# Matmuls without a reader on TensorE in the norms and at the layer edges of a two-block transformer kernel

## The chip, the cores and the metric

The kernel is one program on one core of a Trainium2 chip. Its metric is the device time of one launch in microseconds (us), of which the median over several executions counts. TensorE (PE in the profile) does the matmuls, VectorE (DVE), ScalarE (ACT) and GpSimd (POOL) the elementwise work, and SyncE (SP) starts the DMAs.

## The reference

Two blocks of two layers each work on 512 tokens of 1024 features, in float32. Each layer begins with an RMS norm, and each MLP, and the gate at the end of a layer of the first block, has a norm of its own:

```python
def _rms_norm(x, g):
    xf = x.astype(jnp.float32)
    y = xf * lax.rsqrt(jnp.mean(xf * xf, axis=-1, keepdims=True) + EPS) * g.astype(jnp.float32)

for l in range(DEPTH):                       # first block, DEPTH = 2
    h = _rms_norm(x, in_norm_g[l]); y = h @ w_in[l] + b_in[l]
    ...                                      # mLSTM, HGRN2 and sliding-window attention
    x = x + jnp.concatenate([m_out, h_out, s_out], axis=-1) @ w_out[l]
    u = _rms_norm(x, mlp_norm_g[l]) @ w_up[l]
    x = x + jnp.square(jax.nn.relu(u)) @ w_down[l]
    gate = jax.nn.sigmoid(_rms_norm(x, ple_norm_g[l]) @ w_ple_gate[l])
    x = x + gate * _rms_norm(p[l] @ w_ple_proj[l], ple_post_norm_g[l])
for layer in range(DEPTH):                   # second block
    h = rmsnorm(x, g_attn[layer]) * (1.0 + scale1) + shift1
    x = x + gate1 * mixer_layer(h, w_in[layer], ...)
    h = rmsnorm(x, g_mlp[layer]) * (1.0 + scale2) + shift2
    x = x + gate2 * (gated convolved MLP of h)
return rmsnorm(x, g_final)
```

That makes eleven norms over the whole of x: three per layer of the first block, two per layer of the second, and the last one.

## The kernel before

The activations x stay in SBUF as 8 chunks of 128 features by 512 tokens. Every dense product is made of three matmuls in place of one: weights and activations are split into a high and a low part (fp32r), and high times high, high times low and low times high are summed in PSUM. Weights come in panels of 1 MB; ScalarE writes a panel's high part (L291) and VectorE its low part (L303).

A layer of the first block is four blocks of code (`nc.Block`): the mixer (in `layer_one`), `mlp_one`, `embedding_gate` and `clear_semaphores`. A layer of the second is `layer_two`, `mlp_two` and `clear_semaphores`. Each kind of layer is the body of a hardware loop of two turns (L510 and L1641). At the end of each block of code each engine drains (a DRAIN in its queue) and then all wait for one another; in the profile these instructions bear the line of the `with nc.Block()` (L631, L1394, L1523 for the end of `embedding_gate`, L2163 for that of `mlp_two`, L209 for that of `clear_semaphores`). `clear_semaphores` sets some 60 to 130 semaphores to zero, a fifth of them on each engine; TensorE's are line 233.

A norm crosses such an end. While the last products of a block are added to x, ScalarE squares each chunk (L337) and GpSimd sums the squares (L349). TensorE sums over the partitions with 8 short matmuls (`sum_partitions`, L355 and L358), and its block ends there. In the next block ScalarE takes the root (`root_of_mean`, L362), VectorE the reciprocal (L367), and TensorE, which waits for that, spreads the result over all partitions (`spread_rstd`, L375). Then VectorE scales chunk after chunk (L401), ScalarE makes the high part (L388), VectorE the low part (L408 or L410), and TensorE's first two dense groups (`project_as_ready`, L434) take each chunk when it is ready: 48 matmuls. After that TensorE goes on with L420, L445 and the others.

For the first norm of a layer, `clear_semaphores` and the jump of the loop lie between the sum and the root, and VectorE splits a weight panel between the chunks (L303, before chunks 1 and 4 of the scaling). In `embedding_gate` TensorE's first products after the spread are those of the embedding (L420 on `ple_p_high`), which wait for a DMA, a copy and a subtraction (L1564, L1599).

Of the kernel before, what the change touches and what calls it, by code (L numbers as in the profile page):

```python
# [21 lines left out]
P = 128  # L22
# [180 lines left out]
        return self.made[name]  # L203

def clear_semaphores(nc, s):

    sems = list(s.made.values())
    with nc.Block() as block:  # L209
        @block.gpsimd  # L210
        def _(pool):
            for sem in sems[0::5]:
                pool.sem_clear(sem)

        @block.sync
        def _(sp):
            for sem in sems[1::5]:
                sp.sem_clear(sem)

        @block.vector  # L220
        def _(dve):
            for sem in sems[2::5]:
                dve.sem_clear(sem)

        @block.scalar
        def _(act):
            for sem in sems[3::5]:
                act.sem_clear(sem)

        @block.tensor  # L230
        def _(pe):
            for sem in sems[4::5]:
                pe.sem_clear(sem)

class Panels:
# [115 lines left out]
def sum_partitions(nc, pe, g, e):  # L352
    pe.wait_ge(e.sum_used, DC - 1)
    for t in range(NT):
        nc.tensor.matmul(g.bank[0][:, t:t + 1], g.rstd[:, 1, t * P:(t + 1) * P], g.ones[:, 0:1], start=t == 0, stop=False)  # L355
    pe.wait_ge(e.sq_ready, DC)
    for t in range(NT):
        nc.tensor.matmul(g.bank[0][:, t:t + 1], g.sq[:, (DC - 1) % 2, t * P:(t + 1) * P], g.ones[:, 0:1], start=False, stop=t == NT - 1)  # L358
# [9 lines left out]
    dve.wait_ge(e.rstd_spread, 1)  # L368

def spread_rstd(nc, pe, g, e):

    pe.wait_ge(e.rstd_ready, 1)
    for t in range(NT):
        ins = nc.tensor.matmul(g.bank[0][:, t * P:(t + 1) * P], g.by_token[:, NT + t:NT + t + 1].broadcast_to([P, P]), g.ident, start=True, stop=True)  # L375
    ins.then_inc(e.rstd_spread, 1)

def norm_scalar(nc, act, g, e, high, shift=None, before=None, shifts_ready=None):
# [134 lines left out]
def layer_one(nc, g, a, s, pan, l, k1, vec, row, gb, cs, lb, lsel, small):  # L514
    bank, x, nb = g.bank, g.x, g.nb
    with ExitStack() as ctx:
# [81 lines left out]
        e, nx = NormSignals(s, "in"), NormSignals(s, "mlp")  # L598
# [32 lines left out]
        with nc.Block() as block:  # L631
# [16 lines left out]
            def _(pe):  # L648
# [175 lines left out]
                        ins = nc.tensor.transpose(bank[7][:, t * P:(t + 1) * P], mix_chunk(c, t), g.ident)  # L824
                    ins.then_inc(chunk_turned, 1)

                spread_rstd(nc, pe, g, e)
                for i in range(n_before):
                    dense(i)
                for k in range(n_levels):  # L830
# [534 lines left out]

    mlp_one(nc, g, s, pan, l, vec)
    embedding_gate(nc, g, a, s, pan, l, vec)
    clear_semaphores(nc, s)

def mlp_one(nc, g, s, pan, l, vec):
# [134 lines left out]
def embedding_gate(nc, g, a, s, pan, l, vec):  # L1506
# [5 lines left out]
    e, ee, nx = NormSignals(s, "ple"), NormSignals(s, "emb"), NormSignals(s, "in")  # L1512
    with ExitStack() as ctx:
# [9 lines left out]
        with nc.Block() as block:  # L1523
            @block.sync
            def _(sp):
                sp.dma_start(pT[:, :, :], a["p1"][l, :, :, :]).then_inc(s("ple_in"), 16)
                pan.loads(sp, l, first + AHEAD, first + 5 + AHEAD)
                pan.load_next_layers(sp, l)

            @block.tensor  # L1530
            def _(pe):
                spread_rstd(nc, pe, g, e)
                w = pan.parts(pe, first)
                pe.wait_ge(s("p_low"), 1)
                for c in range(DC):
                    grp.free(pe, c)
                    project_feature(nc, pe, w, c * P, (ph, pl), grp.bank(g, c), kts=2).then_inc(full, 1)
                for c in range(DC):
                    w = pan.parts(pe, first + 1 + c // 2)
                    grp.free(pe, DC + c)  # L1540
                    if c == 0:
                        grp.free(pe, DC + 1)
                        project_as_ready(nc, pe, w, (hh, hl), [grp.bank(g, DC), grp.bank(g, DC + 1)], full, e.h_ready)
                    if c >= 2:
                        project_feature(nc, pe, w, (c % 2) * P, (hh, hl), grp.bank(g, DC + c)).then_inc(full, 1)
                    if c == 0:
                        pe.wait_ge(ee.sum_used, DC)
                        nc.tensor.matmul(g.bank[7][:, :], g.ones, erstd[:, 1, :], start=True, stop=True).then_inc(s("emb_total"), 1)
                sum_partitions(nc, pe, g, nx)

            @block.gpsimd
            def _(pool):
                for c in range(1, DC):
                    pool.wait_ge(ee.sq_ready, c + 1)
                    if c > 1:
                        pool.wait_ge(ee.sum_used, c)
                    nc.gpsimd.tensor_tensor(erstd[:, 1, :], esq[:, 0, :] if c == 1 else erstd[:, 1, :], esq[:, c, :], ALU.add).then_inc(ee.sum_used, 2 if c == 1 else 1)
                add_squares(nc, pool, g, nx)

            @block.scalar  # L1560
            def _(act):
                def p_high():
                    act.wait_ge(s("ple_in"), 16)
                    nc.scalar.activation(ph[:, :, :], pT[:, :, :], ACT.Copy).then_inc(s("p_high"), 1)  # L1564

                def embedding(c):
                    act.wait_ge(full, c + 1)
                    nc.scalar.activation(emb[:, c, :], grp.bank(g, c)[:, :], ACT.Copy).then_inc(s("emb_kept"), 1)
                    act.wait_ge(s("emb_kept"), c + 1)
                    nc.scalar.activation(esq[:, c, :], emb[:, c, :], ACT.Square).then_inc(ee.sq_ready, 1)  # L1570

                norm_scalar(nc, act, g, e, hh, before={0: p_high, 2: lambda: embedding(0), 3: lambda: embedding(1), 4: lambda: embedding(2),
                                                       5: lambda: embedding(3), 6: lambda: embedding(4), 7: lambda: embedding(5)})
                embedding(6)
                embedding(7)
                pan.high(act, first + 2)
                pan.high(act, first + 3, full, DC)
                for c in range(DC):
                    if c == 2:
                        pan.high(act, first + 4, full, DC + 2)  # L1580
                    act.wait_ge(full, DC + c + 1)
                    if c >= 2:
                        act.wait_ge(s("x_gated"), c - 1)
                    nc.scalar.activation(gate[:, c % 2, :], grp.bank(g, DC + c)[:, :], ACT.Sigmoid).then_inc(s("gate_kept"), 1)
                    if c == 0:
                        act.wait_ge(s("emb_total"), 1)
                        nc.scalar.activation(erstd[:, 0, :], g.bank[7][:, :], ACT.Sqrt, bias=g.eps, scale=1.0 / D).then_inc(ee.root_ready, 1)
                    if c >= 1:
                        act.wait_ge(s("x_gated"), c)
                        square_chunk(nc, act, g, nx, c - 1, x[:, c - 1, :])  # L1590
                act.wait_ge(s("x_gated"), DC)
                square_chunk(nc, act, g, nx, DC - 1, x[:, DC - 1, :])

            @block.vector
            def _(dve):
                st = Steps(s("ple_steps")).on(dve)
                def p_low():
                    dve.wait_ge(s("p_high"), 1)
                    nc.vector.tensor_tensor(pl[:, :, :], pT[:, :, :], ph[:, :, :].bitcast(F32), ALU.subtract).then_inc(s("p_low"), 1)  # L1599

                norm_vector(nc, dve, g, e, x, vec[:, V_GPLE:V_GPLE + DC], hh, hl, before={0: p_low})
                pan.low(dve, first + 2)
                dve.wait_ge(ee.root_ready, 1)
                st.link(nc.vector.reciprocal(erstd[:, 1, :], erstd[:, 0, :]))
                pan.low(dve, first + 3)
                for c in range(DC):
                    if c == 2:
                        pan.low(dve, first + 4)
                    st(nc.vector.scalar_tensor_tensor(emb[:, c, :], emb[:, c, :], vec[:, V_GPOST + c:V_GPOST + c + 1], erstd[:, 1, :], ALU.mult, ALU.mult))
                    dve.wait_ge(s("gate_kept"), c + 1)  # L1610
                    st.settle()
                    st.link(nc.vector.tensor_tensor(gate[:, c % 2, :], gate[:, c % 2, :], emb[:, c, :], ALU.mult))
                    nc.vector.tensor_tensor(x[:, c, :], x[:, c, :], gate[:, c % 2, :], ALU.add).then_inc(s("x_gated"), 1)
# [57 lines left out]
def layer_two(nc, g, a, s, pan, l, k2, vec, row, fb, mod, small):  # L1671
    bank, x, nb = g.bank, g.x, g.nb
    with ExitStack() as ctx:
# [90 lines left out]
        e = NormSignals(s, "in")  # L1764
# [18 lines left out]
        with nc.Block() as block:  # L1783
# [16 lines left out]
            def _(pe):  # L1800
# [90 lines left out]
                        ins = nc.tensor.transpose(bank[7][:, t * P:(t + 1) * P], mix_chunk(c, t), g.ident)  # L1891
                    ins.then_inc(chunk_turned, 1)

                spread_rstd(nc, pe, g, e)
                for i in range(n_before):
                    dense(i)
                for i in range(n_steps):
# [234 lines left out]
                    dense(i)  # L2132

    mlp_two(nc, g, s, pan, l, vec, mod)
    clear_semaphores(nc, s)

def mlp_two(nc, g, s, pan, l, vec, mod):
# [15 lines left out]
    e, nx = NormSignals(s, "mlp"), NormSignals(s, "in")  # L2154
    with ExitStack() as ctx:
# [7 lines left out]
        with nc.Block() as block:  # L2163
# [6 lines left out]
            def _(pe):  # L2170
                spread_rstd(nc, pe, g, e)
                for i, (half, kind, c, part) in enumerate(calls):
# [18 lines left out]
                                                   start=part == 0 and k == 0 and q == 0, stop=part == 1 and k == rows[1] - 1 and q == 2)  # L2191
                    ins.then_inc(full, 1)
                sum_partitions(nc, pe, g, nx)

            @block.gpsimd
            def _(pool):
# [226 lines left out]
```

## Time and profile before

| | |
|---|---|
| runs | 3159.9, 3160.41, 3169.08 us; median 3160.41 |
| profiled execution | 3157.43 us, span 3155.6 us |
| mean granted TensorE clock | 0.951 of full |
| PE busy | 2879.8 us (91%), 14756 matmuls |
| DVE busy | 1667.7 us (53%) |
| ACT busy | 1106.7 us (35%) |
| POOL busy | 108.0 us (3%) |
| DMA | 89 GB/s on average |

The granted clock is a share of full speed: 1.00 is 2.4 GHz and 0.50 is 1.2 GHz, and the chip grants TensorE no other level in this trace. A row of the timeline gives the start, the time from the start of the first to the end of the last of a merged group, the engine, the line, the operation, and in brackets how long the engine was idle before it and what ended that. The end of a matmul's record is modelled: two matmuls that follow one another overlap in the records, and the distance of their starts is what each costs.

### The profile page before, as it was taken

The numbers are of one execution on the slowest core, as the hardware profiler recorded it, in microseconds if no ns is written. First come the engines' busy times: TensorE is split into PE (matmuls) and PEld (weight loads), VectorE is DVE, ScalarE is ACT, GpSimd is POOL, SyncE is SP. The second block draws the span as 40 slices with busy tenths as digits, with TensorE's granted clock in tenths as the row PEclk, the third lists the DMA queues.
The fourth block names the chain that finished last, engine by engine and source line by source line (L and its number), as shares of the span: only waits on it lengthen the run. The fifth ranks groups of instructions, "written<-read, shape, count | busy, mean of one in ns | idle before, by whom it ended". The sixth has DMA issues, their size and how long they took to land. (4 is left out here: it accounts for less than half of the span.)

```text
span 3155.6 us, 37966 instructions
## 1 busy us (share of the span) xinstructions
PE 2879.8 (91%) x14756; PEld 2346.2 (74%) x14756; DVE 1667.7 (53%) x3011; ACT 1106.7 (35%) x1691; POOL 108.0 (3%) x88
## 2 busy tenths in 40 slices
PE   4798999999787989999996998899998998999998
PEld 3676778887666867888875887788886786778886
DVE  3656575555657555656655544553444544454442
ACT  4334332223453343222243444332332344332231
POOL 1000000000200000000020000000000000000000
PEclk9988899999888978999998999999998999999999
DMA  3110144443121102444422210132322210122322
GB/s 133 64 44 27 47 143 158 160 160 140 60 81 45 54 27 75 166 160 173 153 80 95 81 40 28 54 107 75 110 77 94 81 53 19 64 81 82 112 77 77
DMA packets 42993, 280.86 MB, mean 89 GB/s; under 512 B 5944, under 2 KB 6200, under 8 KB 11704
## 3 DMA queue, kind: packets, MB, share of 16 engines
q1 hardware_dynamic: 42808, 278.34, 25.4%
q8 instruction: 122, 2.00, 0.2%
q14 instruction: 63, 0.52, 0.1%
HBM read 276.23 MB, written 2.10 MB: 88 GB/s over the span
## 5 line engine op out<-in xcount | busy, mean ns | idle before, releaser
L303 DVE TENSOR_TENSOR low_panels<-raw_panels,high_panels 128x2048 fp32r<-128x2048 f32 (+3 forms) x218 | 469.2, 2153 | 345.1 <-ACT high_panels L291 345.0
L291 ACT ACTIVATE high_panels<-raw_panels 128x2048 fp32r<-128x2048 f32 (+3 forms) x218 | 392.5, 1801 | 494.9 <-PE bank L1419 150.6
L420 PE MATMUL bank<-mlp_h_high,high_panels 128*128 128x512 f32 x1152 | 457.3, 397 | 0.0
L420 PE MATMUL bank<-mlp_h_low,high_panels 128*128 128x512 f32 x1152 | 455.2, 395 | 0.0
L420 PE MATMUL bank<-mlp_h_high,low_panels 128*128 128x512 f32 x1152 | 455.1, 395 | 0.0
L420 PEld LDWEIGHTS bank<-mlp_h_high,low_panels 128*128 128x128 f32 x1152 | 216.1, 188 | 52.6
L420 PEld LDWEIGHTS bank<-mlp_h_low,high_panels 128*128 128x128 f32 x1152 | 216.2, 188 | 51.5
L420 PEld LDWEIGHTS bank<-mlp_h_high,high_panels 128*128 128x128 f32 x1152 | 216.2, 188 | 51.5
L445 PE MATMUL bank<-high_panels,h_high 128*128 128x256 f32 x704 | 211.6, 301 | 13.3 <-DVE arena L1100 12.7
L420 PE MATMUL bank<-h_high,high_panels 128*128 128x512 f32 x496 | 207.7, 419 | 12.9 <-DVE arena L1080 12.8
L1419 PE MATMUL bank<-mlp_hid_high,high_panels 128*128 128x512 f32 x512 | 204.5, 399 | 0.0
L445 PE MATMUL bank<-low_panels,h_high 128*128 128x256 f32 x704 | 202.4, 287 | 0.0
L1419 PE MATMUL bank<-mlp_hid_low,high_panels 128*128 128x512 f32 x512 | 202.4, 395 | 0.0
L1419 PE MATMUL bank<-mlp_hid_high,low_panels 128*128 128x512 f32 x512 | 202.3, 395 | 0.0
L445 PE MATMUL bank<-high_panels,h_low 128*128 128x256 f32 x704 | 201.6, 286 | 0.0
L420 PE MATMUL bank<-h_low,high_panels 128*128 128x512 f32 x496 | 199.1, 401 | 0.0
L420 PE MATMUL bank<-h_high,low_panels 128*128 128x512 f32 x496 | 198.4, 400 | 0.0
L1480 DVE SCALAR_TENSOR_TENSOR mlp_mod_acc<-raw_panels,conditioning,mlp_mod_acc 128x256 f32<-128x256 f32 x336 | 165.1, 491 | 12.0
L445 PEld LDWEIGHTS bank<-high_panels,h_high 128*128 128x128 f32 x704 | 138.2, 196 | 34.9 <-issue 19.8
L1963 ACT ACTIVATE masked_scores<-masked_scores,stats 128x128 f32<-128x128 f32 (+3 forms) x160 | 81.3, 555 | 216.7 <-DVE stats L2067 216.7
L445 PEld LDWEIGHTS bank<-low_panels,h_high 128*128 128x128 f32 x704 | 138.5, 197 | 1.5 <-issue 1.4
L2190 PE MATMUL bank<-mlp_hid_high,high_panels 128*128 128x512 f32 x352 | 139.0, 395 | 0.0
(344 smaller groups left out, 4900.5 us busy)
## 6 DMA issues: line engine op xcount, KB each, us to landing
raw_panels<-in_w SPq DMA_DIRECT2D x238, 1024.0 KB, 4.9
raw_panels<-in_w SPq DMA_DIRECT2D x16, 384.0 KB, 3.2
raw_panels<-in_w SPq DMA_DIRECT2D x4, 960.0 KB, 4.6
raw_panels<-in_w SPq DMA_DIRECT2D x4, 768.0 KB, 4.2
row<-in_row SPq DMA_DIRECT2D x2, 1220.0 KB
x<-in_xT SPq DMA_DIRECT2D x1, 2048.0 KB, 7.6
raw_panels<-in_w SPq DMA_DIRECT2D x4, 512.0 KB, 3.5
mix<-in_rope SPq DMA_DIRECT2D x2, 1024.0 KB, 7.7
```

Of the source, the lines that this page charges most:

```text
L291: self.nc.scalar.activation(self.g.high[:, i % SPLIT, 0:raw.shape[1]], raw, ACT.Copy).then_inc(self.high_ready, 1)
L303: self.nc.vector.tensor_tensor(self.g.low[:, i % SPLIT, 0:w], raw, self.g.high[:, i % SPLIT, 0:w].bitcast(F32), ALU.subtract).then_inc(sel ...
L420: ins = nc.tensor.matmul(bank[:, :], w[a][:, k, c0:c0 + P], rhs[b][:, k0 + k, :], start=first and k == 0 and j == 0, stop=last and k == kt ...
L445: ins = nc.tensor.matmul(bank[:, 0:n], rhs[b][:, k, t * P:(t + 1) * P], w[a][:, k, :], start=k == 0 and j == 0, stop=k == DC - 1 and j == 2)
L1419: ins = nc.tensor.matmul(b[:, :], w[a_][:, k, (m % 2) * P:(m % 2 + 1) * P], (uh, ul)[b_][:, k, :], start=k == 0 and j == 0, stop=k == DC - ...
L1480: ins = nc.vector.scalar_tensor_tensor(o, w[:, k, :], g.cond[:, k:k + 1], o, ALU.mult, ALU.add)
L1963: nc.scalar.activation(o, o, ACT.Exp, bias=g.negmax[:, 2 * i + m:2 * i + m + 1], scale=u.scale).then_inc(w.probs_ready, 1)
L2190: ins = nc.tensor.matmul(b[:, :], w[a_][:, k, (c % 2) * P:(c % 2 + 1) * P], (uh, ul)[b_][:, k0 + k, :], start=part == 0 and k == 0 and q = ...
```

## The change

A new function issues n float32 matmuls of 128 by 128 by 128 (the matrix of ones against the identity) into PSUM bank 7. Nothing reads what they write. They wait for nothing and signal nothing. The change puts them in five places: 6 ahead of the wait for the reciprocal in each `spread_rstd`; 7 behind the spread (14 in the first norm of a layer); 10 behind the partition sums at the end of `embedding_gate`; 10 at the end of `mlp_two`; and 10 behind TensorE's share of `clear_semaphores`.

```diff
-def clear_semaphores(nc, s):
+def clear_semaphores(nc, g, s):
...
             for sem in sems[4::5]:
                 pe.sem_clear(sem)
+            keep_running(nc, g, 10)
...
-def spread_rstd(nc, pe, g, e):
-
+def keep_running(nc, g, n):
+
+    for _ in range(n):
+        nc.tensor.matmul(g.bank[7][:, 0:P], g.ones, g.ident, start=True, stop=True)
+
+
+def spread_rstd(nc, pe, g, e, n_after=7):
+
+    keep_running(nc, g, 6)
     pe.wait_ge(e.rstd_ready, 1)
     for t in range(NT):
         ins = nc.tensor.matmul(g.bank[0][:, t * P:(t + 1) * P], ...)
     ins.then_inc(e.rstd_spread, 1)
+    keep_running(nc, g, n_after)
...
-                spread_rstd(nc, pe, g, e)              # in layer_one and in layer_two
+                spread_rstd(nc, pe, g, e, 14)
...
                 sum_partitions(nc, pe, g, nx)          # in embedding_gate and in mlp_two
+                keep_running(nc, g, 10)
```

## Rows read from the trace of the kernel before

**Rows 1.** Page, part 2: granted TensorE clock in 40 slices, tenths of full

```profile
PEclk9988899999888978999998999999998999999999
```

**Rows 2.** Page, part 5: busy us, mean ns | idle us before it

```profile
L420 PE MATMUL bank<-mlp_h_high,high_panels 128*128 128x512 f32 x1152 | 457.3, 397 | 0.0
```

**Rows 3.** Timeline, norm ahead of the MLP, first layer: start, us, engine, line

```profile
402.81 1.78 PE L375 MATMUL bank<-kc,norm_by_token 128*128 128x128 f32 x8 [2.09 <-DVE norm_by_token L367]
...
406.80 0.75 DVE L401 SCALAR_TENSOR_TENSOR norm_buffers<-x,vec,bank 128x512 f32<-128x512 f32 x1
...
406.91 0.77 PE L434 MATMUL bank<-mlp_h_high,high_panels 128*128 128x512 f32 x1 [2.32 <-DVE mlp_h_low L408]
...
407.48 0.63 PE L434 MATMUL bank<-mlp_h_low,high_panels 128*128 128x512 f32 x1
...
407.90 0.63 PE L434 MATMUL bank<-mlp_h_high,low_panels 128*128 128x512 f32 x1
...
408.18 0.75 DVE L401 SCALAR_TENSOR_TENSOR norm_buffers<-x,vec,bank 128x512 f32<-128x512 f32 x1
...
410.26 0.40 PE L434 MATMUL bank<-mlp_h_high,low_panels 128*128 128x512 f32 x1
...
410.49 0.40 PE L434 MATMUL bank<-mlp_h_high,high_panels 128*128 128x512 f32 x1
```

**Rows 4.** Stretches, L434 alone: length, PE busy (count), PEld, clock, DMA, GB/s

```profile
2765.70:2772.00 6.30, 6.17 (x15) 4.84 (x16) 0.50 0.01 3
```

**Rows 5.** Stretches, all engines: PE, PEld, DVE, ACT, POOL busy, clock, DMA

```profile
1109.80:1113.10 3.30, 3.30 (x25) 2.97 (x25) 0.00 (x0) 1.19 (x2) 0.00 (x0) 0.50 0.00 0
...
1113.20:1116.50 3.30, 2.00 (x24) 1.25 (x20) 1.07 (x8) 1.44 (x3) 0.00 (x0) 1.00 0.00 0
...
782.10:792.20 10.10, 5.79 (x15) 4.50 (x15) 6.28 (x9) 4.30 (x7) 0.00 (x0) 0.50 0.11 42
...
850.30:870.70 20.40, 6.64 (x23) 5.62 (x23) 7.32 (x10) 7.31 (x8) 0.13 (x1) 0.50 0.54 171
```

**Rows 6.** Line L1523, 848 to 852 us: duration ns, first and last start

```profile
L1523 ACTq DRAIN  x1: 659/659/659, 849.3 to 849.3; - x1
L1523 PEldq DRAIN  x1: 1563/1563/1563, 850.0 to 850.0; - x1
```

**Rows 7.** Line L209, 853 to 856 us, the same columns

```profile
L209 DVEq DRAIN  x1: 19/19/19, 854.0 to 854.0; - x1
L209 PEldq DRAIN  x1: 13/13/13, 855.0 to 855.0; - x1
```

**Rows 8.** Timeline, first block, edge between its two layers

```profile
849.94 1.56 PE L358 MATMUL bank<-kc,norm_buffers 128*128 128x1 f32 x8 [0.16 <-ACT norm_buffers L337]
...
860.86 2.07 PE L375 MATMUL bank<-kc,norm_by_token 128*128 128x128 f32 x8 [9.36 <-DVE norm_by_token L367]
...
874.07 0.50 PE L434 MATMUL bank<-h_high,high_panels 128*128 128x512 f32 x1 [0.72 <-DVE h_low L408]
```

**Rows 9.** Line L510, the first block's loop, 855 to 860 us

```profile
L510 PEldq COMPARE_BRANCH  x1: 3317/3317/3317, 855.4 to 855.4; - x1
```

**Rows 10.** Line L1641, the second block's loop, 2414 to 2420 us

```profile
L1641 PEldq COMPARE_BRANCH  x1: 3767/3767/3767, 2414.6 to 2414.6; - x1
```

**Rows 11.** Timeline, second block, edge between its two layers

```profile
2411.35 1.03 PE L358 MATMUL bank<-kc,norm_buffers 128*128 128x1 f32 x8
...
2419.43 2.08 PE L375 MATMUL bank<-kc,norm_by_token 128*128 128x128 f32 x8 [7.04 <-DVE norm_by_token L367]
```

**Rows 12.** Timeline, norm ahead of the gate, first layer

```profile
781.00 1.16 PE L375 MATMUL bank<-kc,norm_by_token 128*128 128x128 f32 x8 [0.81 <-DVE norm_by_token L367]
...
786.47 0.76 PE L420 MATMUL bank<-ple_p_high,high_panels 128*128 128x512 f32 x1 [4.32 <-DVE ple_p_low L1599]
```

**Rows 13.** Timeline, the last norm

```profile
3143.66 1.28 ACT L362 ACT_TABLE_LOAD   x1 [3.74 <-PEq L209]
...
3145.48 2.08 PE L375 MATMUL bank<-kc,norm_by_token 128*128 128x128 f32 x8 [3.94 <-DVE norm_by_token L367]
```

More of the change, by code:

```diff
@@ L1367, in layer_one @@
     embedding_gate(nc, g, a, s, pan, l, vec)
-    clear_semaphores(nc, s)
+    clear_semaphores(nc, g, s)
 def mlp_one(nc, g, s, pan, l, vec):
@@ L1892, in turn_chunk @@
                     ins.then_inc(chunk_turned, 1)
-                spread_rstd(nc, pe, g, e)
+                spread_rstd(nc, pe, g, e, 14)
                 for i in range(n_before):
@@ L2134, in layer_two @@
     mlp_two(nc, g, s, pan, l, vec, mod)
-    clear_semaphores(nc, s)
+    clear_semaphores(nc, g, s)
 def mlp_two(nc, g, s, pan, l, vec, mod):
@@ L2193, in _ @@
                 sum_partitions(nc, pe, g, nx)
+                keep_running(nc, g, 10)
             @block.gpsimd
```

## The prediction

> **What bounds the kernel now.** I read the page first. TensorE is busy for 91% of the span, and the largest groups of matmuls have no idle time before them [rows 2], so in the dense stages TensorE sets the time: each microsecond that it gains or loses there is gained or lost at the end. Its granted clock is full in most slices but dips in some [rows 1]. The timeline and the table of stretches say where. In the norm ahead of the first MLP, TensorE ends its partition sums, has nothing for about 2 us, runs the spread, has nothing for 2.3 us more, and starts the products at half clock: the starts of L434 are 0.42 us apart at first and 0.23 us apart from 410 us on [rows 3]. In the fourth such norm the stretch has a clock of 0.50 and lasts longer [rows 4]. So a matmul of 512 columns costs 0.19 us more at half clock. At the loop's edge the clock is 0.50 for 20 us [rows 5]. Last, the ends of the blocks: which engine drains last there decides when all go on.
>
> **MLP norms (four).** The 6 ahead of the spread stand where TensorE waited 2.09 us for the reciprocal, of which the end of the block takes about 0.25, so 1.85 us are free. They fit at full clock; at half they make the spread 0.7 us late. The 7 behind it stand in the 2.3 us up to the first chunk: they fit at full clock and cost 0.7 us at half. If the clock holds, the spread takes 0.9 us less than at half and L434 none at half clock. The four sites had 7, 7, 8 and 14 such matmuls, 36 in all (the last site, the longest of the four, stands in [rows 4]); at 0.19 us that is 6.9 us; with some 0.8 us for each spread, 3.2 us, the most is 10.1 us. VectorE begins a chunk each 1.38 us [rows 3] and TensorE needs 6 × 0.233 = 1.40 us for it, so VectorE does not take the gain back. The least is a loss of 4 × 1.4 = 5.6 us. I take a gain of 7.8 us, nearer to the most: L358's 8 matmuls have one column each and are little work, and in some sites the sums, the end of the block and this gap will still pull the clock down before the added ones count.
>
> **Gate norms (two).** TensorE had 0.8 us between the sums and the spread [rows 12], some 0.2 of it the end of the block, so the 6 make the spread late by 0.8 us at full or 2.0 at half. The next products wait for `ple_p_low` until 786.47, 4.3 us after the spread, so both this and the 7 (1.6 us) are hidden at full clock; at half they end about 1.2 us late. 13 of the products ran at half clock in each of the two sites (one of the two is the stretch from 782.10 in [rows 5]): 26 × 0.19 = 5.0 us are the most, a loss of 2.4 us the least. I take a gain of 3.7 us: the gap behind the 7 is still 2.6 us.
>
> **First norms of layers (four: at the start and at three edges).** Here a clock at full buys nothing behind the spread. TensorE has to wait at its fourth chunk anyway, for 0.72 us [rows 8], since VectorE splits a panel in between, and eight matmuls at half clock (1.5 us) only fill part of the wait that would then be longer. The 14 have 4.4 us between the spread and the first chunk: 3.2 us at full, 6.0 at half. They follow 6 others and the spread without much of a gap, so I expect the clock to be up in time: 0, with 1.6 us per site as the other bound.
>
> **The tens at the four edges.** These are behind no wait, so nothing hides them. At the end of `embedding_gate` TensorE's drain starts at 850.0 and takes 1.56 us, ScalarE's is over 1.6 us earlier [rows 6]; all others have drained too. So TensorE is the last already, and ten matmuls behind its sums move the end of the block by their whole length. The same holds in `clear_semaphores`: TensorE drains at 855.0, VectorE at 854.0 [rows 7], because TensorE's clears are the slowest. Its ten come behind them, so they too count in full. ScalarE's root, VectorE's reciprocal and SP's DMAs for the next layer are all queued behind that barrier. Term by term:
> - After the first block's two layers, L358 is at half clock (1.56 us for 8, against 1.03 at full [rows 8, 11]) and the clock stays at half from there to the products (last stretch of [rows 5]). Both tens mostly at half: 2 × (4.2 + 4.0) = 16.4 us, with 9.2 and 17.2 as bounds. In the loop's jump TensorE's own branch takes 3.3 us and ends at 858.74 [rows 9]; the spread starts 2.1 us later [rows 8], so 6 at half clock are 0.5 us late.
> - Between the second block's layers the sums still ran at full clock [rows 11]: 3.0 and 3.5 us, bounds 4.6 and 8.6 for both. The branch ends at 2418.36 [rows 10], the spread started 1.07 us later [rows 11], so the 6 make it late by 0.3 us at full and 1.5 at half. After 4 us without a matmul I take 1.5. Together 8.0 us.
> - After the last layer: 2.9 and 2.6 us. The 6 have 1.8 us from the barrier [rows 13] and fit at full clock (0.8 us late at half); the spread is then up to 0.9 us shorter, of which I take 0.6. Together 4.9 us.
> The edges cost 16.4 + 0.5 + 8.0 + 4.9 = 29.8 us.
>
> **The sum.** 29.8 − 7.8 − 3.7 = +18.3 us on 3157.43 us, which is 3175.7 us. The median of the runs is 3 us over the profiled execution; with the same shift I write 3178 us. All at full clock the sum would be 8 × 2.3 + 0.3 − 0.9 × 3 − 10.1 − 5.0 = +0.9 us. All at half it would be 8 × 4.3 + 0.5 + 1.5 + 0.8 + 4 × 1.6 + 5.6 + 2.4 = +51.6 us.
>
> **A rule of the skill.** In the trace, a stretch of 3.3 us at half clock with nothing but dense float32 work against the identity is followed by one at full clock (the first two of [rows 5]). Part of that work is transposes by TensorE (L769), part plain matmuls against the identity (L772). The Trainium skill, "TensorE: Matmul & The Clock Gate", section "PE-mode transpose", says that the clock gate doesn't engage for transposes, as they do not count as busy in the same way. The trace speaks against carrying that over to the added matmuls, which are plain ones; if they too did not count, it would be the first rival below.
>
> **Rivals.**
> - *The added matmuls do not move the clock.* Then nothing is gained and all cost half-clock prices where the clock is low: the tens 34 us less a few, the lateness some 8 us, +42 us in all: 3200 us. Against it stands the stretch above. Chance 0.06.
> - *The clock holds at full nearly everywhere*, at the edges too: the tens keep it up through the clears. About +1 to +6 us: 3164 us. The 4 us in which TensorE's branch runs speak against it at two edges, sums that already end at half clock [rows 8] at the two of the first block. Chance 0.12.
> - *The edges turn out free and the kernel gets faster.* The mechanism would be that something else ends the barriers: if the next layer's start waited for a DMA or for the fetch of instructions that runs on while TensorE multiplies, the tens would be covered as the 7 are. Then −11.5 us and up to 3 for the late spreads: 3150 us. It decides once the cover at an edge passes 4 us of the 8. The drains speak against it: TensorE's is the last in both blocks. Chance 0.07.
> - *My forecast*, 0.75, with 3168 to 3188 us as its own range.
>
> **How the numbers follow.** A measurement of this kernel tells a difference of about 0.3%, 9.5 us, from none. The forecast lies 18 us above the median, and of its own range a small part is below 3170. Slower: 0.75 × 0.95 + 0.06 = 0.77. Faster: the third rival, whose price lies just beyond 9.5 us, for two thirds, 0.05. Within: the rest, 0.18. The range goes from 3160, most of the second rival, to 3192, short of the first.
>
> **What would show it.** After: more than 1.00 us between TensorE's and the other drains at both lines of the edges, some 4 us each in the first block; L434 at 0.23 us from its first on in at least two of four MLP norms; a mean clock above 0.951; and the next layer's root starting about 8 us later after the sums in the first block, 6 in the second. I am wrong if the barrier at an edge is ended by another engine than TensorE, or if L434 still starts at half clock in all norms.

## The result and the profile after

The changed kernel took 3187.36 us (median of 5 runs, 3181.7 to 3196.49) against 3160.41 (5 runs, 3155.87 to 3169.08). The ratio is 1.0084, with a 95% interval from 1.0060 to 1.0108: 0.8% slower. The prediction said slower, at 3178 us, and its range of 3160 to 3192 holds the time. The mean granted clock rose from 0.951 to 0.958, and the kernel is slower all the same. The profiled execution had a span of 3185.6 us, against 3155.6.

Here is part 2 of the page after, to be read against [rows 1], and the group that answers to [rows 2]. The dense products cost what they cost before.

```profile
PEclk9988999999898989999997999999999999999999
...
L429 PE MATMUL bank<-mlp_h_high,high_panels 128*128 128x512 f32 x1152 | 458.6, 398 | 0.0
```

To see where 30 us of span went, I cut both traces at TensorE's first partition sum and at its last early product (L434 before, L443 after) of each norm. "Norm" below is the time from the first to the last of these, "stage" the time from there to the next sums.

| part | before | after | difference | predicted |
|---|---|---|---|---|
| first norm, at the start | 36.0 | 38.0 | +2.0 | 0 to 1.6 |
| MLP norms (4) | 85.4 | 76.4 | −9.0 | −7.8 |
| rest of the first block's MLP stages (2) | 716.4 | 722.3 | **+6.0** | 0 |
| gate norms (2) | 67.8 | 62.7 | −5.1 | −3.7 |
| four edges, three with the first norm behind them, the last up to its spread | 107.3 | 144.7 | **+37.4** | +30.4 |
| from the last spread on | 10.2 | 9.2 | −0.9 | −0.6 |
| attention stages (4) | 1318.6 | 1318.4 | −0.3 | 0 |

The differences are of the unrounded times. The rows of the table make +30.1 us where the spans differ by 29.9. What is left out of it did not move by more than 0.2 us.

Two rows lean on these two executions. The fourth MLP norm of this profile of before took 22.3 us, the other three 20.9 to 21.1; in the five profiles below that are without the 6 and 7, the four norms took 83.9 to 85.4 us, so the gain is 7.5 to 9.0 us. And the first norm, in `after_late_mod`, where its code is that of the changed kernel, took 35.9 us and not 38.0: its +2.0 is not a fixed cost of the 14.

**MLP norms.** The timeline of the norm ahead of the first MLP, as in [rows 3] (start, duration, engine, line). The 6 are done 0.21 us before the spread, the spread takes 1.16 us instead of 1.78, the wait behind the 7 is 0.76 us instead of 2.32, and from its second on L443 starts 0.23 us apart:

```profile
404.54 1.16 PE L383 MATMUL bank<-kc,norm_by_token 128*128 128x128 f32 x8 [0.21 <-DVE norm_by_token L368]
405.53 1.73 PE L375 MATMUL bank<-kc 128*128 128x128 f32 x14
408.01 0.47 PE L443 MATMUL bank<-mlp_h_high,high_panels 128*128 128x512 f32 x1 [0.76 <-DVE mlp_h_low L417]
408.33 0.39 PE L443 MATMUL bank<-mlp_h_low,high_panels 128*128 128x512 f32 x1
408.55 0.40 PE L443 MATMUL bank<-mlp_h_high,low_panels 128*128 128x512 f32 x1
```

**What the first block's MLP gives back.** Further on in the same timeline, TensorE first. It reaches its matmuls on a modulation panel (L1435) early, and waits 1.52 us for VectorE's chain of eight instructions. Then the clock falls: L429 starts 0.43 us apart, for eight matmuls.

```profile
419.01 0.40 PE L443 MATMUL bank<-mlp_h_high,low_panels 128*128 128x512 f32 x1
420.92 0.61 PE L1435 MATMUL bank<-kc,mlp_mod_acc 128*128 128x1 f32 x4 [1.52 <-DVE mlp_mod_acc L1489]
421.39 0.48 PE L429 MATMUL bank<-mlp_h_high,high_panels 128*128 128x512 f32 x1
...
422.28 0.63 PE L429 MATMUL bank<-mlp_h_high,high_panels 128*128 128x512 f32 x1
422.70 0.63 PE L429 MATMUL bank<-mlp_h_low,high_panels 128*128 128x512 f32 x1
...
425.59 0.39 PE L429 MATMUL bank<-mlp_h_high,low_panels 128*128 128x512 f32 x1
```

VectorE in that stretch, where its chunks and the chain follow one another without a gap:

```profile
415.49 1.48 DVE L417 TENSOR_TENSOR mlp_h_low<-norm_buffers,mlp_h_high 128x512 fp32r<-128x512 f32 x2
416.88 0.35 DVE L1486 TENSOR_SCALAR mlp_mod_acc<-raw_panels,conditioning 128x256 f32<-128x256 f32 x1
417.26 3.61 DVE L1489 SCALAR_TENSOR_TENSOR mlp_mod_acc<-raw_panels,conditioning,mlp_mod_acc 128x256 f32<-128x256 f32 x7
```

The kernel before had the same chain, over at 419.76 us, the moment at which TensorE's last early product was over too. So TensorE came to it with no wait. The changed kernel's norm is 2.05 us shorter, but the chain ends only 0.6 us earlier after the sums (20.9 us against 21.5), so most of what the faster norm gives ends in the wait:

```profile
416.15 3.61 DVE L1480 SCALAR_TENSOR_TENSOR mlp_mod_acc<-raw_panels,conditioning,mlp_mod_acc 128x256 f32<-128x256 f32 x7
...
419.36 0.40 PE L434 MATMUL bank<-mlp_h_high,low_panels 128*128 128x512 f32 x1
419.82 0.61 PE L1426 MATMUL bank<-kc,mlp_mod_acc 128*128 128x1 f32 x4
```

**The edges.** The drains (duration in ns, first and last start in us) at the edge between the first block's layers, against [rows 6, 7]. The first is the block's end, the second that of the clears; the semaphore event is the barrier's release.

```profile
L1532 PEldq DRAIN  x1: 3433/3433/3433, 852.9 to 852.9; - x1
L1532 PEldq EVENT_SEMAPHORE  x1: 51/51/51, 856.5 to 856.5; - x1
...
L209 DVEq DRAIN  x1: 19/19/19, 858.8 to 858.8; - x1
L209 PEldq DRAIN  x1: 4048/4048/4048, 860.3 to 860.3; - x1
```

Each barrier is released right behind TensorE's drain, 3 to 6 us behind the end of the last of the others. Reckoned from ScalarE's drain, the first release is 4.7, 4.4, 4.0 and 4.5 us later than before at the four edges (17.6), and the second comes 4.5, 4.4, 2.5 and 3.9 us later behind the first one (15.4). The tens together cost 32.9 us in this execution. The edges as a whole took 9.9, 11.7, 7.4 and 8.5 us more, so 0.7, 2.8, 0.9 and nothing are left beside the tens. The timeline of the first edge shows what is behind it:

```profile
867.88 1.28 ACT L363 ACT_TABLE_LOAD   x1 [17.82 <-issue]
868.58 2.63 PEld L375 LDWEIGHTS bank<-kc 128*128 128x128 f32 x12 [4.58 <-issue]
868.58 2.93 PE L375 MATMUL bank<-kc 128*128 128x128 f32 x12 [4.29 <-issue]
...
869.54 0.18 DVE L368 RECIPROCAL norm_by_token<-norm_by_token 128x4 f32<-128x4 f32 x1 [20.15 <-ACT norm_by_token L363]
...
871.30 1.68 PE L383 MATMUL bank<-kc,norm_by_token 128*128 128x128 f32 x8
```

TensorE's branch is over at 868.52, and the 6 run at half clock from 868.58 to 871.3, though the reciprocal was ready at 869.7: the spread is 1.5 us late. At the products the clock is up, but TensorE then has to wait at the fourth chunk for VectorE, for 2.32 us where it was 0.72 [rows 8]:

```profile
884.12 0.50 PE L443 MATMUL bank<-h_high,high_panels 128*128 128x512 f32 x1 [2.32 <-DVE h_low L417]
```

There the clock stays up: the starts behind it are 0.23 us apart. At the start and at the edge between the blocks it falls after a wait of about the same length (2.32 and 2.43 us), for 8 products. That is 1.4 us of the second edge; the other 1.4 us of it lie between the barrier and the spread, where VectorE's reciprocal stands behind its instruction L2121, which waits for a DMA (3.91 us, 3.21 before).

### The profile page after: what moved, and what is told of

Same layout as the page of the kernel before. It is cut to its first block and busy times, and to the rows that moved or that the text cites. A ratio compares the mean times of both kernels' runs of the same rounds, so it can differ in the third digit from the quotient of the medians.

```text
span 3185.6 us, 38970 instructions
## 1 busy us (share of the span) xinstructions
PE 2947.2 (93%) x15258; PEld 2413.7 (76%) x15258; DVE 1666.9 (52%) x3011; ACT 1106.4 (35%) x1691; POOL 107.9 (3%) x88
## 3 DMA queue, kind: packets, MB, share of 16 engines
q8 instruction: 125, 2.05, 0.3%
## 5 line engine op out<-in xcount | busy, mean ns | idle before, releaser
L429 PE MATMUL bank<-mlp_h_high,high_panels 128*128 128x512 f32 x1152 | 458.6, 398 | 0.0
L429 PE MATMUL bank<-mlp_h_high,low_panels 128*128 128x512 f32 x1152 | 456.4, 396 | 0.0
L429 PE MATMUL bank<-mlp_h_low,high_panels 128*128 128x512 f32 x1152 | 456.2, 396 | 0.0
L429 PEld LDWEIGHTS bank<-mlp_h_high,low_panels 128*128 128x128 f32 x1152 | 216.8, 188 | 53.0
L429 PEld LDWEIGHTS bank<-mlp_h_low,high_panels 128*128 128x128 f32 x1152 | 217.1, 188 | 51.7
L429 PEld LDWEIGHTS bank<-mlp_h_high,high_panels 128*128 128x128 f32 x1152 | 216.9, 188 | 51.7
L429 PE MATMUL bank<-h_high,high_panels 128*128 128x512 f32 x496 | 208.1, 419 | 11.4 <-DVE arena L1089 11.2
L1428 PE MATMUL bank<-mlp_hid_high,high_panels 128*128 128x512 f32 x512 | 204.5, 399 | 0.0
L1428 PE MATMUL bank<-mlp_hid_high,low_panels 128*128 128x512 f32 x512 | 202.3, 395 | 0.0
L429 PE MATMUL bank<-h_low,high_panels 128*128 128x512 f32 x496 | 199.7, 403 | 0.0
L429 PE MATMUL bank<-h_high,low_panels 128*128 128x512 f32 x496 | 199.0, 401 | 0.0
L2200 PE MATMUL bank<-mlp_hid_high,low_panels 128*128 128x512 f32 x352 | 139.0, 395 | 0.0
```

Of the source, the lines that this page charges most:

```text
L429: ins = nc.tensor.matmul(bank[:, :], w[a][:, k, c0:c0 + P], rhs[b][:, k0 + k, :], start=first and k == 0 and j == 0, stop=last and k == kt ...
L1428: ins = nc.tensor.matmul(b[:, :], w[a_][:, k, (m % 2) * P:(m % 2 + 1) * P], (uh, ul)[b_][:, k, :], start=k == 0 and j == 0, stop=k == DC - ...
L2200: ins = nc.tensor.matmul(b[:, :], w[a_][:, k, (c % 2) * P:(c % 2 + 1) * P], (uh, ul)[b_][:, k0 + k, :], start=part == 0 and k == 0 and q = ...
```

## The experiments

The kernel before was run beside each group of kernels, 17 or 23 times; its medians were 3164.05, 3162.81 and 3164.19 us. The profiled execution of before was thus one of its shorter ones. The attention stages show why: they took 1318.6 us in it and 1330.1 us in that of `inner_norms`, with the same instructions there. TensorE's clock was at half for 177.5 us of them in the one and for 201.4 us in the other. A single profile is good for a stage, not for the last 12 us of the whole.

A difference in us behind a ratio is that ratio less one, times the median of before of its group. The plain difference of the two medians is up to 3 us off it, which is less than the width of the intervals.

### Which part costs, which part gains

`edges_only`: no `keep_running` in `spread_rstd`.

```
 def spread_rstd(nc, pe, g, e, n_after=7):
-    keep_running(nc, g, 6)
     pe.wait_ge(e.rstd_ready, 1)
...
-    keep_running(nc, g, n_after)
```

> Only the ten matmuls at both places of the four edges are left; the 6, 7 and 14 of the norms are out. Theory A (the tens are the loss, TensorE's drain ends both barriers at every edge): the edges took 36.6 us more in the profile with the whole change, of which some 1.5 us per edge come from the 6 and up to 1.4 from the chunk at which the products wait for VectorE. Without those about +30 us on 3160: 3190, between 3184 and 3196, and the MLP norms take 21 us each as before. Rival B (the 6 and 14 of the first norms are a large part of the loss): under 3180. Rival C (the tens alone also mend the norms' clock): under 3182, with MLP norms near 19 us.

Measured: 3196.69 us, ratio 1.0103 (1.0088 to 1.0117), +32.6 us. The MLP norms took 21.09, 21.08, 20.98 and 21.00 us. Theory A holds, B and C fall: the tens are the whole loss, and they do nothing for the norms.

`norms_only`: the tens out at the three places (`-keep_running(nc, g, 10)`), the rest left.

> The tens are out, all of the 6, 7 and 14 stay. Theory A: MLP norms -9.0, gate norms -5.0, the rest of the first block's MLP stage +6.0 (TensorE waits for VectorE's modulation chain, then runs at half clock), first norms of layers +1 to +2 each: -3 us, 3157, between 3152 and 3162. Rival B: over 3170. Rival D (the tens were needed to bring the clock up for the 6): the norms gain nothing, 3165 or more.

Measured: 3161.89 us, 0.9992 (0.9983 to 1.0002), −2.5 us. MLP norms at 19.03 to 19.08 us, so D falls, and B with it (over 3170); the first block's MLP stages at 361.15 and 361.17 us.

`inner_norms`: as that, and nothing in the first norms of layers either.

```
-                spread_rstd(nc, pe, g, e, 14)
+                spread_rstd(nc, pe, g, e, 0, 0)
```

> Only the 6 and 7 of the four MLP norms and the two gate norms; nothing at the edges and in the first norms of layers. Theory A: -9.0 - 5.0 + 6.0 = -8 us: 3152, between 3148 and 3157, and 3 to 7 us below norms_only. Theory of my prediction (VectorE takes nothing back): -14 us, 3146. Rival D: no less than 3160.

Measured: 3160.14 us, 0.9987 (0.9978 to 0.9996), −4 us. The norms gain their 14 us (76.3 us for the four MLP norms, 62.7 for the gates), but the stages behind them are at 361.15 and 361.13 us. Theory A's −8 lies just outside the interval (−7.0 to −1.3), my prediction's −14 far outside. The parts in the profiles make −8, and where the other 4 us are is open; the next kernel's −14.6 fits its parts. The 6 and 14 of the first norms cost less than I expected, 1.7 us between the two medians. The two profiles do not settle it: the first norm and the edges took 7.0 us more in that of `norms_only` (155.5 against 148.4), the attention stages 9.1 us less.

### Where the gain of the norms goes

`inner_late_mod`: `inner_norms` with this edit in `mlp_one`. TensorE's matmuls on a modulation panel come one call, 24 matmuls, later.

```
-                    if m % 2 == 1:
-                        for n in range(pan.upto(p + AHEAD), ...
+                    if m % 2 == 0 and i > 0:
+                        for n in range(pan.upto(p - 1 + AHEAD), ...
```

> As inner_norms, with TensorE's eight matmuls on each modulation panel in the first block's MLP one call (24 matmuls of 512 columns) later. Theory E (TensorE's wait for the modulation chain, and the half clock that follows it, are what takes the gain back): the MLP stage after the norm is 3 us shorter in each of the two layers: 3146, some 6 us below inner_norms, no wait at the modulation matmuls. Rival F (VectorE's chain sets the pace of this stage, wherever TensorE waits for it): the wait only moves to the next products, and the time is that of inner_norms within 1.5 us.

Measured: 3151.26 us, 0.9954 (0.9941 to 0.9967), −14.6 us. The stages fell to 357.84 us, both of them, 3.3 us less each. VectorE's chain stands as it did (416.27 us, 3.61 long), and TensorE now has dense products across its end at 419.9 us and comes to the modulation matmuls without a wait, at full clock:

```profile
419.64 0.40 PE L428 MATMUL bank<-mlp_h_high,high_panels 128*128 128x512 f32 x1
419.88 0.40 PE L428 MATMUL bank<-mlp_h_low,high_panels 128*128 128x512 f32 x1
...
423.84 0.50 PE L1434 MATMUL bank<-kc,mlp_mod_acc 128*128 128x1 f32 x4
424.21 0.47 PE L428 MATMUL bank<-mlp_h_high,high_panels 128*128 128x512 f32 x1
```

The time fell by 8.9 us between the two medians, of which the stages make 6.6. Theory E holds and F falls: VectorE was not the pace of this stage, only one wait stood in it.

`late_mod_alone`: the same edit, with nothing of the change.

> Nothing of the change is in; only TensorE's matmuls on each modulation panel come one call later. Theory E (the wait arises only because the norm ahead has become 2 us faster, and before there was none): 0 us, between -1.5 and +1.5, and the stage behind the norm takes 358.2 us as before, or 0.3 us less. Rival J (the late matmuls are a gain of their own, apart from the norms, and account for the 8.9 us between inner_norms and inner_late_mod): -6 us or more.

Measured: 3162.25 us, 0.9997 (0.9988 to 1.0005), no difference; stages of 357.84 and 357.85 us, 0.3 us less each than before. J falls: the edit has next to nothing to mend where the norm is slow.

`after_late_mod`: the same edit in the whole change.

> The whole change, with the modulation matmuls one call later. Theory E: the stage behind the MLP norm in the first block takes 357.8 us instead of 361.2, twice: 6.6 us below the changed kernel, +20.5 us on before. Rival F' (with the tens in, the clock falls there for another reason): still 361 us, +27.

Measured: 3184.71 us, 1.0074 (1.0059 to 1.0089), +23.4 us (20.5 between the medians); stages of 357.84 us, both, so F' falls. That the time fell by 6.6 us too is not settled: the intervals of this ratio and of the changed kernel's overlap.

`inner_late_six`: `inner_late_mod` without the 7 (`n_after=0`).

> As inner_late_mod, without the 7 behind the spread. Theory K (both are needed: the 6 bring the clock up for the spread, but the 2.3 us without a matmul between it and the first product let it fall again): MLP norms at 20.2 to 20.5 us with 7 or 8 products at half clock, so that 1.2 us of the 2.0 of each are lost, gate norms a little longer or equal: +5 us on inner_late_mod, 3156. Rival L (the 6 do it alone): MLP norms at 19.1 us, the time that of inner_late_mod.

Measured: 3162.24 us, 0.9994 (0.9985 to 1.0004), −1.9 us. MLP norms at 20.44 to 20.64 us, gate norms at 32.9 and 32.8, the stages still at 357.84: 1.5 us lost in each MLP norm and 1.4 in each gate norm, 8.6 us in all. K's mechanism holds and L falls. The loss is larger than I expected: the gate norms lose too, and the time is 11 us above that of `inner_late_mod` where I had put 5. Its rows have the spread at full clock and the fall behind the gap:

```profile
405.26 1.16 PE L382 MATMUL bank<-kc,norm_by_token 128*128 128x128 f32 x8 [0.21 <-DVE norm_by_token L367]
408.73 0.47 PE L442 MATMUL bank<-mlp_h_high,high_panels 128*128 128x512 f32 x1 [2.32 <-DVE mlp_h_low L416]
409.04 0.54 PE L442 MATMUL bank<-mlp_h_low,high_panels 128*128 128x512 f32 x1
409.38 0.63 PE L442 MATMUL bank<-mlp_h_high,low_panels 128*128 128x512 f32 x1
```

### The price of a place

`block_ten_only`: only the tens behind the sums.

> Only the ten matmuls at the end of embedding_gate and of mlp_two (four edges), nothing else of the change. In the profile of the whole change the first of the two barriers came 4.7, 4.6 and 4.0 us later after the sums at three edges, some 4.3 at the last. Theory A (each ten costs its own length behind TensorE's drain, and the two tens add up): +17.6 us, between 14 and 21. Rival G (each pair shares a cost, because what follows has slack for one of them): under 10 us here while both together cost 32.6.

Measured: 3176.51 us, 1.0048 (1.0035 to 1.0060), +15.2 us, as theory A has it. TensorE's four drains took 4.05, 4.05, 3.02 and 2.18 us.

`clear_ten_only`: only the tens behind the clears.

> Only the ten matmuls behind TensorE's clears. In the profile of the whole change the second barrier came 4.5, 4.5, 2.1 and about 3.3 us later. Theory A: +14.4 us, between 11 and 18, the four drains of TensorE at 4.05, 4.05, 2.2 and 3.3 us. Rival H (the ten ahead of them had held the clock up for these): without that ten all four drains take 4 us or more, and the cost is 17 us. Rival G: under 10 us.

Measured: 3176.48 us, 1.0050 (1.0036 to 1.0065), +15.8 us. G falls: 15.2 and 15.8 make 31.0, where both together cost 32.6; theory A's cost holds, and its drains do in the first block. H falls as I wrote it, since the four drains took 4.05, 4.05, 3.37 and 3.79 us and not 4 us or more each. Whether the first ten makes the second cheaper at all, the runs do not tell. At the edge between the second block's layers the drain took

```profile
L209 PEldq DRAIN  x1: 3373/3373/3373, 2427.3 to 2427.3; - x1
```

without the other ten ahead of it. With it, the changed kernel has

```profile
L209 PEldq DRAIN  x1: 2175/2175/2175, 2435.5 to 2435.5; - x1
```

and `edges_only` has

```profile
L209 PEldq DRAIN  x1: 3437/3437/3437, 2444.8 to 2444.8; - x1
```

At the last edge it was 3.79 us without the other ten, and 3.32 us in the changed kernel and 2.17 us in `edges_only` with it. So TensorE's drain behind ten of them takes 2.2 to 4.05 us in the second block, and differs between executions of the same matmuls.

`inner_late_ten_in_wait`: ten in `embedding_gate`, ahead of the sums.

```
+                for _ in range(10):
+                    nc.tensor.matmul(g.bank[0][:, P:2 * P], g.ones, g.ident, start=True, stop=True)
                 sum_partitions(nc, pe, g, nx)
```

> As inner_late_mod, with ten matmuls at each edge of the first block ahead of its sums, in TensorE's 2.5 us wait for GpSimd's squares, where the change has them behind the sums. Theory A (the price of the tens is their place behind the last wait, not their number): 0 us, -0.5 per edge if the sums are then at full clock (8 matmuls in 1.03 instead of 1.56 us), the spread and the products behind the edge at half clock as before, since TensorE has nothing for 8 us between. Rival M (ten matmuls there bring the sums late or hold the clock across the edge): +2 us or more at the sums, or a spread at 1.1 us.

Measured: 3148.68 us, 0.9955 (0.9941 to 0.9969), the time of `inner_late_mod`. The same twenty records that cost 4.4 to 4.7 us behind the sums cost nothing here: they end 0.32 us before GpSimd's squares are there. The sums are at full clock (1.05 us, not 1.56 [rows 8]), and 8.6 us later the spread is at half clock, as before:

```profile
841.99 2.39 PE L1558 MATMUL bank<-kc 128*128 128x128 f32 x20
844.70 1.05 PE L355 MATMUL bank<-kc,norm_buffers 128*128 128x1 f32 x8 [0.32 <-POOL norm_buffers L349]
845.91 1.05 PE L358 MATMUL bank<-kc,norm_buffers 128*128 128x1 f32 x8 [0.16 <-ACT norm_buffers L337]
855.56 2.08 PE L382 MATMUL bank<-kc,norm_by_token 128*128 128x128 f32 x8 [8.60 <-DVE norm_by_token L367]
```

Theory A holds, M falls.

`clears_shared`: the kernel before, with a third of TensorE's clears on SP.

```
-            for sem in sems[1::5]:
+            for sem in sems[1::5] + sems[4::5][::3]:
...
-            for sem in sems[4::5]:
+            for sem in [x for i, x in enumerate(sems[4::5]) if i % 3]:
```

> Nothing of the change is in; each third of TensorE's semaphore clears is given to SP. Theory A also says that the second barrier hangs on TensorE's clears alone, 1 us behind VectorE's: with 7 or 5 fewer of them it comes 0.8 to 1.0 us earlier at each edge, -3.5 us in all, 3160.5 against 3164. Rival I (another engine or SP's loads end the edge anyway): the barrier moves, the root does not, 0 us. In the time alone -3.5 us is near what can be told; the profile's barrier tells.

Measured: 3164.51 us, 1.0002 (0.9993 to 1.0011). TensorE's drain is no longer the last one, VectorE's is:

```profile
L209 PEldq DRAIN  x1: 13/13/13, 856.9 to 856.9; - x1
L209 DVEq DRAIN  x1: 19/19/19, 857.1 to 857.1; - x1
```

Its second barrier came 1.0, 1.2, 0.3 and 0.7 us earlier after the sums than before, so it did hang on TensorE's clears, and the root came 0.7 to 1.7 us earlier, against rival I. The four edges took 105.1 us in its profile against 107.3; at the third the reciprocal came 1.1 us later all the same, behind an instruction of VectorE's that waits for a DMA (2.16 us, 0.70 before). But −3.5 us lies outside the interval of the time (−2.2 to +3.5 us): theory A's amount fails. Whether the edges' 2 us are in the time is open, since the interval holds both −2 and nothing.

`inner_late_shared`: the later modulation matmuls and the shared clears, both on `inner_norms`.

> inner_late_mod with each third of TensorE's clears on SP: the candidate for the best version. In clears_shared VectorE's drain had become the last of that barrier (TensorE's had been 1.0 us later than it before), and the time did not move by more than 0.1%. Expected: inner_late_mod's time less 0 to 4 us, 3149. Rival I: the same as inner_late_mod.

Measured: 3149.53 us, 0.9957 (0.9942 to 0.9973). It can't be told from `inner_late_mod` (0.9954), nor can `inner_late_ten_in_wait`. These three are the best versions, 0.45% faster than before and some 1.3% faster than the change as it was made. The plain `inner_late_mod`, the simplest of them, is the one to keep.

## Why the prediction was right, and where it was off

- *TensorE ends both barriers at each edge, so the tens count in full*: shown, by the drains and by `edges_only`, `block_ten_only` and `clear_ten_only`. The bare tens were put at 8.2, 8.2, 6.5 and 5.5 us; they measured 9.1, 8.8, 6.5 and 8.5, in all 4.5 us more. The size was off most at the last edge, where I took full clock for both: its two drains took 4.05 and 3.3 us. In `edges_only`, with the same tens, both took 2.17 us there, full clock as I had it, so this part of the miss is of the execution.
- *The 6 at the edges are 0.5 us late in the first block*: too low, 1.5 us at the first edge. I had the branch and the root keep their distance; TensorE's branch now took 3.79 us instead of 3.32 [rows 9], while ScalarE's table came 0.4 us sooner after the barrier. Between the second block's layers I took 1.5 us, and the spread came 0.8 us after its reciprocal was ready.
- *A full clock in the first norms of layers buys nothing, 0 to 1.6 us*: right in kind. VectorE's panel split holds the fourth chunk, so what TensorE gains before it turns into a longer wait (0.72 to 2.32 us). The start took 2.0 us more, above my bound; in another execution of the same code it took no more than before. At the edge between the blocks eight products at half clock behind that wait cost 1.4 us.
- *MLP norms −7.8 us*: −9.0 in this profile, four times at full clock from the first product. Part of this is the fourth norm, slow in this profile of before; against the other kernels without the 6 and 7 the gain is 7.5 us and up, which is the forecast. `inner_late_six` shows that the 7 are worth about 1.5 us of the 2 that a site gains.
- *Gate norms −3.7 us*: −5.1; the 6 ran partly at half clock there and made the spread late, as thought, but the gap for `ple_p_low` covers it. Of that gap 0.45 us were left behind the 7, not 2.6: I had subtracted the 7 and forgotten the late spread. The products started at full clock all the same, so the gain came to my bound of 5.0.
- *VectorE does not take the gain back*: this step failed. I compared the pace of chunks, 1.38 us against TensorE's 1.40, and stopped at the eighth. Behind it VectorE has the modulation chain of 4.0 us, TensorE waits for that at L1435, and a wait of 1.5 us is followed by eight matmuls at half clock. I had put this term at nothing. It cost 3.3 us in each of the first block's two layers (361.15 to 357.84 us), 6.6 in all, more than those two norms had gained (4.1). `inner_late_mod` against `inner_norms` shows it, `late_mod_alone` that there was nothing to gain before.
- *The rule on transposes*: the added matmuls are plain ones, and they do move the clock. The norms at full clock speak for this in all kernels with the 6 and 7, so the first rival falls, and the section "PE-mode transpose" of the Trainium skill's page "TensorE: Matmul & The Clock Gate" is no obstacle here. No run here shows what it says of transposes themselves. The same page's section "Loop structure matters more than you think" calls a loop good in which VectorE copies a result out of PSUM between TensorE's dense groups, whose matmuls follow at once, and says that this does not break TensorE's warmth. Here TensorE had to wait for VectorE's work at 420.92, and the matmuls behind it fell to half clock; with the same work and no wait, in `inner_late_mod`, they did not.
- *The second rival* (full clock nearly everywhere, +1 to +6) falls by the drains of 4.05 us; *the third* (edges covered, faster) by all kernels with tens behind the sums or the clears.
- *The signs I named*: the mean clock rose (0.958), L443 was at full clock in all four MLP norms, TensorE's drains ended every barrier, and at the first edge ScalarE's table load, with the root behind it, came 8.8 us later after the sums, for a forecast of 8; between the second block's layers it was 5.9 us, for 6.

The forecast of 3178 was 9 us below the median of 3187. On the profiled execution the sum was +18.3 us, and 29.9 were measured. The edges' 37.4 instead of 30.4 and the unseen 6.0 and 2.0 us are 15.0 too much; the norms' −14.1 instead of −11.5, the attention stages and the tail take 3.2 of that back. The right answer thus rests on the tens, which are most of the loss, and for the rest on luck: a term of 6.0 us was missing, and the time still lies inside the range, 5 us below its upper end, and only 0.6 us inside the forecast's own 3188. Against the medians of before that were taken beside the experiments the changed kernel is 23 to 25 us slower and not 27, nearer to the forecast; that too is no merit of the sum.

## What to carry to other kernels

Matmuls that only hold the clock are free where TensorE waits for another engine anyway, and are paid in full behind the last wait before a barrier that TensorE ends. In the norms here the group ahead of the spread was not enough: with the 6 alone about 0.5 us of the 2.0 were left in an MLP norm. Whether the 7 behind it would do alone was not tried. Dense work has to follow directly; ten of them ahead of 8.6 us with nothing left the spread at half clock. After TensorE is made faster, look for its next wait on the engine that paced it: here one such wait of 1.5 us took back more than the norm ahead of it had won, and with the waiting matmuls 24 products later the stage took as long as it does with no wait.

## What the runs showed of the hardware

- A wait of 1.5 us in otherwise dense work was followed by eight 512-column matmuls at half clock, twice in each of the three profiles that have the 6 and 7 and the modulation matmuls at their old place. Waits of 0.76 and 0.91 us in the same norms were not.
- The length of a wait does not settle it alone. The waits of 2.3 to 2.4 us at the fourth chunk of the first norms, with the same code, were followed by half clock at all four places in `norms_only`, at two in the changed kernel and at none in `after_late_mod`.
- Ten added matmuls took 2.4 us at full clock (`inner_late_ten_in_wait`), and TensorE's drain with ten ahead of it took from 2.2 to 4.05 us.
- TensorE's branch at the loop took 3.32 us before and 3.79 us after at the same edge, the other engines' 0.07 us and less. What makes it vary was not tried.
- The profile of before was 3 to 7 us below its medians; the attention stages, the same instructions in all kernels, took 1317.8 to 1330.1 us in the fourteen profiles, with the clock at half for 177.5 us of them in the shorter ones and up to 201.4 us in the longer.
